# Block 1: the gains of the features without rotation as a column, in the copy of the turned tiles

## The reference

```python
q = (_rmsnorm(c_q, cq_g) @ w_uq).reshape(bn, s, MLA_HEADS, MLA_QK)      # 8 heads of 96 features
kv = (_rmsnorm(c_kv, ckv_g) @ w_ukv).reshape(bn, s, MLA_HEADS, MLA_NOPE + MLA_V)
k_nope, v = kv[..., :MLA_NOPE], kv[..., MLA_NOPE:]
k = jnp.concatenate([k_nope, k_rope], axis=-1)
q = _rmsnorm(q, q_g)                                                    # over the 96 features, gain q_g
k = _rmsnorm(k, k_g)
q = jnp.concatenate([q[..., :MLA_NOPE], _apply_rope(q[..., MLA_NOPE:], cos, sin)], axis=-1)
k = jnp.concatenate([k[..., :MLA_NOPE], _apply_rope(k[..., MLA_NOPE:], cos, sin)], axis=-1)
o = _chunk_causal_attention(q, k, v)
```

## Time and profile before

| | us |
|---|---|
| runs before | 1651.77, 1651.87, 1654.35; median 1651.87 |
| profiled execution | 1654.05 |
| its span | 1652.2 |
| TensorE busy | 1583.6 (96%) |
| VectorE busy | 912.7 (55%) |
| ScalarE busy | 770.0 (47%) |
| GpSimd busy | 46.7 (3%) |

### The profile page before, as it was taken

The page is one execution under the profiler, slowest core; times in us unless marked ns, Lnnn a source line. Parts: engine busy times, 40 slices in busy tenths (PEclk is TensorE's granted clock), DMA queues, the critical chain, the costliest instruction groups (busy, mean ns, idle before and its releaser), DMA issues.

```text
span 1652.2 us, 22035 instructions
## 1 busy us (share of the span) xinstructions
PE 1583.6 (96%) x8345; PEld 1307.0 (79%) x8345; DVE 912.7 (55%) x1924; ACT 770.0 (47%) x1599; POOL 46.7 (3%) x75
## 2 busy tenths in 40 slices
PE   6999999999999999999999999999999999989999
PEld 6887768788887887777788888898866679977667
DVE  4597546443445379546444335568664464965443
ACT  4443444333334352545333334435667553456772
POOL 0000001000001000001100000100000010000000
PEclk9999999999999999999999999999999999999999
DMA  7232112333332333112233333332212233311121
GB/s 217 87 89 77 51 39 77 92 100 90 90 106 75 98 102 90 52 52 79 65 89 102 99 92 115 99 90 69 70 37 62 75 90 96 96 45 58 40 76 64
DMA packets 80885, 136.07 MB, mean 82 GB/s; under 512 B 8190, under 2 KB 33548, under 8 KB 80780
## 3 DMA queue, kind: packets, MB, share of 16 engines
q1 hardware_dynamic: 77120, 129.22, 26.9%
q10 hardware_dynamic: 3660, 5.44, 1.2%
HBM read 132.55 MB, written 2.10 MB: 81 GB/s over the span
## 4 chain that ended last, share of the span: by engine, by line
PE 82%; DVE 8%; ACT 7%; issue 2%; DMA 0%; ACTq 0%; POOL 0%; DVEq 0%
PE gemm_bank L725 68%; PE aux_bank L851 3%; PE aux_bank L830 2%; PE aux_bank L795 2%; PE aux_bank L811 2%; ACT probs L1160 2%; PE aux_bank L780 1%; DVE w_lo L1466 1%; ACT w_hi L1104 1%; PE aux_bank L839 1%; ACT spread_inv L1174 1%; ACT probsT L1195 1%; DVE rope L1565 1%; DVE probs L1624 1%; PE aux_bank L697 1%
## 5 line engine op out<-in xcount | busy, mean ns | idle before, releaser
L1104 ACT ACTIVATE w_hi<-raw 128x512 fp32r<-128x512 f32 (+3 forms) x524 | 305.1, 587 | 640.9 <-PE gemm_bank L725 640.3
L1466 DVE TENSOR_TENSOR w_lo<-raw,w_hi 128x512 fp32r<-128x512 f32 (+3 forms) x524 | 330.1, 635 | 447.3 <-ACT w_hi L1104 446.2
L725 PE MATMUL gemm_bank<-act_hi,w_hi 128*128 128x512 f32 x768 | 311.1, 405 | 5.4 <-ACT bgT L1417 2.1
L725 PE MATMUL gemm_bank<-act_hi,w_lo 128*128 128x512 f32 x768 | 299.8, 390 | 0.0
L725 PE MATMUL gemm_bank<-act_lo,w_hi 128*128 128x512 f32 x768 | 299.5, 390 | 0.0
L725 PE MATMUL gemm_bank<-w_hi,act_hi 128*128 128x384 f32 (+3 forms) x736 | 266.0, 361 | 1.1 <-DVE qk_c L1506 1.1
L725 PE MATMUL gemm_bank<-w_hi,act_lo 128*128 128x384 f32 (+3 forms) x736 | 257.3, 350 | 0.0
L725 PE MATMUL gemm_bank<-w_lo,act_hi 128*128 128x384 f32 (+3 forms) x736 | 257.2, 349 | 0.0
L725 PEld LDWEIGHTS gemm_bank<-act_hi,w_hi 128*128 128x128 f32 x768 | 144.3, 188 | 43.3 <-issue 11.1
L725 PEld LDWEIGHTS gemm_bank<-act_hi,w_lo 128*128 128x128 f32 x768 | 144.1, 188 | 30.8
L725 PEld LDWEIGHTS gemm_bank<-act_lo,w_hi 128*128 128x128 f32 x768 | 144.5, 188 | 28.6 <-issue 1.0
(11 more groups left out here) (302 smaller groups left out, 2101.2 us busy)
## 6 DMA issues: line engine op xcount, KB each, us to landing
raw<-in_w_in SPq DMA_DIRECT2D x104, 512.0 KB, 3.6
raw<-in_w_in SPq DMA_DIRECT2D x64, 384.0 KB, 3.3
raw<-in_w_out SPq DMA_DIRECT2D x32, 512.0 KB, 3.9
raw<-in_w_branch SPq DMA_DIRECT2D x24, 512.0 KB, 3.8
raw<-in_w_mem_kv SPq DMA_DIRECT2D x8, 512.0 KB, 3.7
raw<-in_w_in SPq DMA_DIRECT2D x16, 256.0 KB, 2.8
raw<-in_w_in SPq DMA_DIRECT2D x8, 416.0 KB, 4.9
x<-in_x SPq DMA_DIRECT2D x4, 512.0 KB, 5.1
```

What stands on the lines that cost most here:

```text
L725: last = pe.matmul(o, a, c, start=begin and n == 0, stop=end and n == 2)
L1104: act.activation(w_hi[:, s % RING, 0:n], raw[:, p % RAW, kk % PIECE, 0:n], ACT.Copy)\
L1466: dve.tensor_tensor(w_lo[:, s % RING, 0:n], raw[:, p % RAW, kk % PIECE, 0:n], w_hi[:, s % RING, 0:n].bitcast(F32), ALU.subtract).then_inc( ...
```

## The change

The gain of the first 64 features is no longer multiplied into q and k before they are turned. It commutes with the turning, since it depends on the feature alone; so it is applied to the turned tile, where a feature is a partition, by the instruction that takes the tile from its bank: a multiplication with a column of `vec_cols` in place of a copy. The column has the gain in its first 64 rows and ones in the 32 behind them (the rotated features have their gain in the rotation's tables, as before). Four rows are added to `vec_rows` for it, q and k of two layers, by three loads: 2 rows of `mla_q_g`, 2 rows of `mla_k_g` and 4 rows of ones. The eight instructions of line 1790 a layer, each with its yield, are gone.

```diff
+    out["k_ones"] = np.ones((2 * DEPTH, P - NOPE), dtype=np.float32)
...
-    R_GATE, R_X, R_MEM, R_POS, R_CQ, R_CKV, R_GLA = 0, 48, 80, 96, 100, 104, 106
-    N_ROWS = 110
+    R_GATE, R_X, R_MEM, R_POS, R_CQ, R_CKV, R_GLA, R_HEAD = 0, 48, 80, 96, 100, 104, 106, 110
+    N_ROWS = 114
...
         rows_at(R_GATE, w["b_gate"]), (inv_freq[:, :], w["k_inv"]),
+        (vec_rows[R_HEAD:R_HEAD + DEPTH, 0:NOPE], w["mla_q_g"][:, 0:NOPE]),
+        (vec_rows[R_HEAD + DEPTH:N_ROWS, 0:NOPE], w["mla_k_g"][:, 0:NOPE]),
+        (vec_rows[R_HEAD:N_ROWS, NOPE:P], w["k_ones"]),
     ]
...
                 bank = aux_wait_full(dve, a.key("q", g, x))
-                dve.tensor_copy(a.qT_of(g, x), bank[0:QK, :]).then_inc(read_of(a.key("q", g, x)), 1)
+                gains = [vec_cols[0:QK, r:r + 1] for r in (R_HEAD + a.l, R_HEAD + DEPTH + a.l)]
+                dve.tensor_scalar(a.qT_of(g, x), bank[0:QK, :], gains[0], None, ALU.mult)\
+                   .then_inc(read_of(a.key("q", g, x)), 1)
                 bank = aux_wait_full(dve, a.key("k", g, x))
-                dve.tensor_copy(a.kT_of(g, x), bank[0:QK, :]).then_inc(read_of(a.key("k", g, x)), 1)
+                dve.tensor_scalar(a.kT_of(g, x), bank[0:QK, :], gains[1], None, ALU.mult)\
+                   .then_inc(read_of(a.key("k", g, x)), 1)
...
                 for tile, gain in ((q, gain_q), (k, gain_k)):
-                    g = gain[:, l, 0:NOPE].unsqueeze(1).to_broadcast([P, MH, NOPE])
-                    settle()
-                    for t in range(NT):
-                        mark(dve.tensor_tensor(tile[:, t, :, 0:NOPE], tile[:, t, :, 0:NOPE], g, ALU.mult))
-                        yield
                     yield from rotate(tile, NOPE, HALF, gain[:, l, :], cos1[:, :, :], sin1[:, :, :], table_1, rope_1, False)
```

## The result

The change makes the kernel slower. The changed kernel takes 1662.47 us (median of 4 runs, 1660.8 to 1663.6), the kernel before 1653.11 us (4 runs too, 1651.77 to 1654.96). The ratio is 1.0050, with a 95% interval of 1.0038 to 1.0063. The forecast was 1651.6, with a range up to 1653.8 and 0.04 for slower.

A forecast was written before the change was run, and what follows sets the result against it. TensorE, busy 96% of the span, was taken as the bound, so only its waits counted. Terms -0.66 - 0.50 + 0 + 0.90 = -0.26 us on the median 1651.87 gave 1651.6 us, range 1650.0 to 1653.8.

The forecast's parts named there:

- Head work, layer 0: Block 1's first layer: head transposes begin at 138.74 instead of 139.40, a gain of 0.66 us.
- the w_lo wait: TensorE's wait for the fifth weights' residue, ahead of the head transposes: claimed to grow from 0.68 to about 1.5 us.
- the signal's: The head transposes' wait for the signal that q and k are finished, 1.6 us a layer: claimed to go in both.
- Layer 1: Same head work sum in block 1's second layer: transposes at 651.90 instead of 652.40, a gain of 0.50 us.
- Copies to multiplications: 32 copies from a bank, 0.055 us more each on VectorE, 1.8 in all; nothing waits, so 0 taken.
- The start: Three loads added last in the first group delay TensorE's first work: 3 x (0.27 + 0.03) = 0.90 us slower.
- my reading: At the start, the last load's landing is counted from its issue, so later issues delay TensorE by 0.90 us.
- rival 2: The start hides the new loads, the landing being held by the bulk loads: 1650.7 us. Chance 0.10.
- Rival 1: Both TensorE waits around the head work go, in both layers: about 5.6 less 0.9 us, giving 1647.2. Chance 0.05.
- The four gaps: Two TensorE waits in each of two layers, 2.6 + 2.5 us, with restarts of 0.14 each about 5.6.
- Rival 3: The new load issues at the start cost 0.67 us each: +0.8 us in all, 1652.7. Chance 0.10.
- Rival 4: Slower: the longer wait at the fifth residue drops TensorE's clock, 5.0 us over two layers, 1656.6. Chance 0.03.

The follow-up runs named there:

- Experiment 1: The kernel before with only the two large areas (branch outputs, merged, head tiles) placed 128 bytes higher: 1663.38 us, ratio 1.0053 to before.
- experiment 11: The changed kernel with the areas 128 bytes higher, matching the weights modulo 256, and plain copies in place of the 32 multiplications: 1654.3 us, ratio 1.0003 to before.
- experiment 2: The changed kernel whole, with the two large areas a further 128 bytes higher so that they match the weights modulo 256: 1653.78 us, ratio 1.0000 to before.
- experiments 1 to 4: Four follow-up kernels on one chip, with the two areas or every tile moved by 128 or 256 bytes; the kernel before had a median of 1654.13 us there.
- experiment 3: The changed kernel with the two large areas a further 256 bytes higher instead of 128, still mismatched with the weights: 1662.18 us, ratio 1.0045 to before.
- experiment 8: The changed kernel at a matching place, with four empty yields for each of q and k in place of the removed multiplications: 1647.5 us, ratio 0.9970 to before.

## Why the prediction was wrong

**The step that failed** is the last sentence on the loads: "The transpose of 114 rows for 110 and the 4 columns more in its copy are nothing." I priced the 4 columns as work, and as work they are nothing. They are also 16 bytes a partition in a memory laid out in order, and these shift two areas by 128 bytes. 1392 matmuls of 512 columns read an operand from there (y 576, merged 384, ya and yb 288, mem 96, c 48), and 96 of 384 columns (c). At 6 ns for each of the 1392, (76.0 − 74.8) / 192 from the rows, that would be 8.4 us. By the starts in the timelines it is 6 ns for y and merged, 5.8 us, and less for the others, 4 for ya, yb and mem and 2 to 5 for c, 2.0 us: together 7.8. Experiment 1, which has this term alone, gives 8.4 to 8.7 when its runs are set against those of before with the same mean clock (1660.29 against 1651.9 at 0.999, 1663.5 against 1654.8 at 0.997). Neither the sum nor any rival had such a term, and the slower rival (the clock) was another mechanism at another place. The address could have been worked out ahead; its price could not, since in the kernel before the operands of all these matmuls match.

**The sum, term by term.**
- Head work, layer 0: −0.66 forecast, −0.24 measured (the lag behind before is 0.47 at 117.18, ahead of the stretch, and 0.23 at 139.40, the transposes). The direction of each wait was right: the w_lo wait rose from 0.68 to 1.69 and the signal's is gone. With the 0.47 taken off, the second residue's step began at 123.23, exactly as worked out; the fifth residue was issued at 132.80 instead of 132.42. The 0.38 are what the rows above show, an idle of 0.41 ahead of u x za, behind the wait for k's last sum that goes with the signal (line 1576), while the sum had set the operations back to back.
- Layer 1: −0.50 forecast, −0.10 measured. The lag went from 5.14 (631.02) to 5.04 (652.40 to 657.44); the same idle of 0.41 is there.
- Copies to multiplications: 0 forecast. One takes 746 ns for 687, as the 742 of the neighbour row said; nobody waits for them, and experiment 11 finds no gain without them.
- The start: +0.90 forecast, +0.62 measured at the first transpose (10.34 to 10.96). The new issues cost 0.32, 0.28 and 0.31, about the 0.30 each that I took. But the last one starts at 6.16, 1.38 behind the last of before and not 0.90: between the two stand the issue of inv_freq (0.67 here, 0.46 before) and two of the new ones. It lands in 4.41 us instead of 5.17. So the landing is in part counted from the issue and in part not: between my reading and rival 2. One pair of executions is a thin base: in the eight profiled ones with the new loads the first transpose comes at 10.92 to 11.69, in the five without at 10.34 to 10.79, and the two means are 0.64 apart.
- Together the terms measure +0.28, against −0.26 forecast, and experiment 2 is that kernel: ratio 1.0000, which can tell neither from 0. So besides the term that it lacked, the sum had the head work 0.8 us too large and the start 0.3.

**The account of the 9.6 us**: the place 7.8, the start 0.6, the head work −0.3 make 8.1. Most of the rest is the clock. Both executions have three stretches at the low level, but at different places. The windows around them (start and end, length, busy us of PE, PEld, DVE, ACT and POOL, granted clock, DMA share, GB/s), first after, then before:

```profile
536.00:544.00 8.00, 7.66 (x34) 7.10 (x35) 5.22 (x9) 2.59 (x5) 0.00 (x0) 0.79 0.71 198
1152.00:1160.00 8.00, 6.26 (x32) 5.81 (x32) 4.08 (x14) 1.46 (x5) 0.00 (x0) 0.79 0.11 34
1596.00:1604.00 8.00, 6.92 (x39) 4.23 (x39) 2.76 (x10) 5.99 (x14) 0.00 (x0) 0.79 0.28 90
```

```profile
16.00:24.00 8.00, 6.88 (x33) 6.21 (x34) 7.87 (x18) 4.56 (x8) 0.00 (x0) 0.79 0.72 177
1284.00:1288.00 4.00, 4.00 (x16) 2.26 (x14) 2.07 (x9) 3.92 (x11) 0.00 (x0) 0.57 0.08 12
1448.00:1456.00 8.00, 6.01 (x32) 5.05 (x31) 4.28 (x14) 1.20 (x3) 0.00 (x0) 0.79 0.07 19
```

Each is a loss of 1.7 us of full clock (8 x 0.21), and laying the two timelines of TensorE side by side shows what it moves: after falls back by 1.5, 1.4 and 1.5 us at its three (the lag goes from 3.55 to 5.01, from 8.23 to 9.60 and from 7.50 to 8.98), and before by 0.4 at the start, and by 1.6 and 1.3 later. Net 1.0, and 8.1 + 1.0 = 9.1; the last 0.5 isn't assigned to anything. The scatter of the times goes with the clock: of before's 19 runs beside experiments 1 to 4 (1651.54 to 1655.84) those with a mean clock of 0.999 took 1651.54 to 1652.76 and those with 0.996 took 1655.08 to 1655.84. The stretches don't follow the place of the areas: experiment 11, with fast matmuls, has them within 8 us of where after has its three (at 532, 1147 and 1590 us), and experiment 3, with slow ones, has a long one at 1270. So about one of the 9.6 us of the profiled pair is the clock of these two executions and not tied to the edit by any run here.

**The rivals.** Rival 1 (both waits go) priced 1647.2. The change doesn't do that, because of its order; experiment 8, which restores the slots, does, at 1647.5. The four gaps were priced at 5.6 us, and the reading of experiment 8 gives 5.9. So the argument against it (larger pieces move up ahead of the late residue) was the right one, and the 4.8 us of VectorE a layer do buy both waits if the slots are kept. Rival 2 (the start hides the loads) is half true at the first transpose, and the total can't tell. Rival 3 (0.67 an issue) is excluded by the three issues themselves, 0.28 to 0.32 each. Rival 4 did not occur: matmuls of 0.39 to 0.40 us stand before and behind the longer wait, and the granted clock is 1.00 from 118 to 146 and from 640 to 660 us. Its price rested on a row that I read wrongly: at 20.91 the clock of before was not "not yet up", it had been at 1.00 from 12 to 16 us and was in the low stretch that began at 18.

**What stays open**: why a mismatch modulo 256 costs, why ya, yb and mem pay less than y and merged and least at 64 bytes, what distances of 16 bytes or of 96 cost, and what decides where the clock falls.

## What to carry to other kernels

A tile that grows moves every tile behind it, so a diff is also a diff of addresses: list the start of each large tile before and after, and keep the two operands of the hot matmuls at the same address modulo 256. When the sum of an engine's busy time rises with the same instructions, compare the same group at the same shape in both traces before looking for waits: 390 to 396 ns for y beside 390 to 391 for act names the cause's place. And where removed pieces let larger ones move up in a hand-made interleaving, keep the empty turns: the same work was worth 5 to 6 us more in its old slots.

## What the runs showed of the hardware

- Matmuls of 512 columns with y or merged, whose two operands in the on-chip memory lie 32, 64 or 128 bytes apart modulo 256, start 0.233 us apart instead of 0.227, and last 394 to 398 ns in the list instead of 389 to 390. With the distance 0 modulo 256 they don't, in any of the layouts tried. Each of six layouts with a mismatch was slower than before in this kernel, by 0.36 to 0.91%.
- The price falls with the width: at 128 bytes apart up to 4 ns in the list for 384 columns (334 to 338 for c, 335 to 339 for act), none for 256 columns (282 and 281) and none for the transposes of 128 (275).
- The clock falls to its low level in stretches that cost 1.3 to 1.6 us each at the five later places read above, and 0.4 at the start; a profiled execution has none to four of them before its last matmul (its mean granted clock is 0.996 to 1.000). Before's scatter of 4 us is of the size of three.
- A multiplication by a column with a bank as source costs 746 ns for 96x512, where the copy costs 687.
- A small load behind the others in the queue of the start landed in 4.41 us, one issued 1.4 us earlier in 5.17: the later issue was paid back for a part. Over all profiled executions the first kind took 4.4 to 5.0 us, the second 5.2 to 5.6.
